# Output projections of a two-layer hybrid kernel: five pairs of tiles in each layer as seven block products instead of eight

## The reference, cut to what matters

```python
for i in range(DEPTH):                       # 2 layers
    y = _even_layer(...) if i % 2 == 0 else _conv_layer(...)   # both end in ... @ w_out
    x = _layernorm(DEEPNORM_ALPHA * x + y, post_ln_g[i], post_ln_b[i])
    x = x + (p[i] @ ple_w[i]) * jax.nn.sigmoid(x @ ple_gate_w[i])
```

## Time and profile before

| what | value |
|---|---|
| median of 3 runs | 2099.53 us (2099.37 to 2099.72) |
| the profiled execution: time | 2099.83 us |
| its span, first to last instruction | 2098.1 us |
| TensorE busy | 2091.8 us |
| VectorE busy | 1256.2 us |
| ScalarE busy | 817.0 us |
| GpSimd busy | 362.0 us |
| DMA, mean over the span | 103 GB/s |

### The profile page before, as it was taken

One profiled execution on the slowest core, in us unless ns is written; L12 is line 12 of the kernel. 1 busy time (PEld: TensorE's weight loads), 2 busy tenths in 40 slices (PEclk: granted clock), 3 DMA queues, 4 the chain that ended last, 5 costly groups with the idle time before them and its releaser, 6 DMA issues.

```text
span 2098.1 us, 28711 instructions
## 1 busy us (share of the span) xinstructions
PE 2091.8 (100%) x10510; PEld 1733.0 (83%) x10510; DVE 1256.2 (60%) x2105; ACT 817.0 (39%) x1042; POOL 362.0 (17%) x196
## 2 busy tenths in 40 slices
...
GB/s 319 141 102 93 70 77 80 80 62 79 81 80 80 60 80 137 133 84 97 99 113 123 135 100 86 96 101 100 100 87 93 100 181 100 92 92 77 142 111 68
DMA packets 33395, 216.76 MB, mean 103 GB/s; under 512 B 3952, under 2 KB 4224, under 8 KB 9520
## 3 DMA queue, kind: packets, MB, share of 16 engines
...
HBM read 207.53 MB, written 8.39 MB: 103 GB/s over the span
## 4 chain that ended last, share of the span: by engine, by line
PE 99%; ACT 1%; DMA 0%; DVE 0%; issue 0%; ACTq 0%
PE G L502 91%; PE X L502 5%; PE T L502 1%; PE T L685 1%; DMA Z<-xT_in 0%; PE T L806 0%; ACT a_hi L917 0%; ACT Z L1112 0%; ACT Y L1184 0%; PE T L811 0%; PE T L657 0%; ACT L1004 0%; DVE tmp L1451 0%; PE T L681 0%; DVE Y L1453 0%
## 5 line engine op out<-in xcount | busy, mean ns | idle before, releaser
L502 PE MATMUL G<-a_hi,w_hi 128*128 128x512 f32 x2764 | 1078.1, 390 | 0.6 <-ACT a_hi L917 0.6
L502 PE MATMUL G<-a_hi,w_lo 128*128 128x512 f32 x2764 | 1072.9, 388 | 0.0
L502 PE MATMUL G<-a_lo,w_hi 128*128 128x512 f32 x2764 | 1070.6, 388 | 0.0
L913 ACT ACTIVATE w_hi<-w_raw 128x2048 fp32r<-128x2048 f32 x173 | 331.5, 1916 | 946.2 <-PE G L502 933.3
L1312 DVE TENSOR_TENSOR w_lo<-w_raw,w_hi 128x2048 fp32r<-128x2048 f32 x128 | 297.1, 2321 | 640.3 <-ACT w_hi L913 640.3
L502 PEld LDWEIGHTS G<-a_hi,w_hi 128*128 128x128 f32 x2764 | 518.9, 188 | 110.3 <-ACT a_hi L917 1.5
L502 PEld LDWEIGHTS G<-a_hi,w_lo 128*128 128x128 f32 x2764 | 518.9, 188 | 107.2 <-issue 0.2
L502 PEld LDWEIGHTS G<-a_lo,w_hi 128*128 128x128 f32 x2764 | 519.0, 188 | 106.4 <-issue 0.5
L1895 DVE SCALAR_TENSOR_TENSOR T<-tmp,par,T 128x512 f32<-128x512 f32 x464 | 306.9, 751 | 0.0
L446 POOL TENSOR_TENSOR w_lo<-w_raw,w_hi 128x2048 fp32r<-128x2048 f32 x45 | 207.8, 4617 | 232.5 <-ACT w_hi L913 232.5
L410 POOL TENSOR_TENSOR a_lo<-Y,a_hi 128x512 fp32r<-128x512 f32 x32 | 44.2, 1397 | 366.9 <-ACT a_hi L917 366.6
...
## 6 DMA issues: line engine op xcount, KB each, us to landing
w_raw<-wall_in SPq DMA_DIRECT2D x174, 1024.0 KB, 4.8
Y<-xT_in POOLq DMA_DIRECT2D x5, 1024.0 KB, 7.2
Y<-w_in POOLq DMA_DIRECT2D x2, 2048.0 KB, 16.0
x_residual<-Y POOLq DMA_DIRECT2D x16, 256.0 KB, 3.8
Y<-x_residual POOLq DMA_DIRECT2D x4, 1024.0 KB, 5.3
out<-Y POOLq DMA_DIRECT2D x15, 256.0 KB, 3.7
w_raw<-wall_in SPq DMA_DIRECT2D x12, 256.0 KB, 7.9
Z<-xT_in SPq DMA_DIRECT2D x6, 512.0 KB, 9.0
```

The lines of the kernel that those rows point to most:

```text
L502: return pe.matmul(o, l, r, start=start, stop=stop)
L913: f(w_hi[:, w.slot, :], w_raw[:, w.slot, :], ACT.Copy).then_inc(S("w_hi"), 1)
```

## The change

Per layer, tiles 0 to 3 are computed as before. Tiles 4 to 13 are taken in five pairs, numbered p = 2 to 6; tiles 14 and 15 (p = 7) are computed in full, but loaded and split in pieces.

In a pair, the first four chunks (`PLAIN_K`) of both tiles are multiplied as before (pieces `r1`, `r2`). The other twelve are seen as 2 x 2 blocks: two tiles by two groups of six chunks on the side of the weights (`b11`, `b21` of the first tile, `b12`, `b22` of the second), two groups of six chunks by two halves of 256 tokens on the side of the activations. The product of such blocks is made with seven products (Winograd's form of Strassen's scheme) instead of eight. It needs four sums of weights, t1 = b11 + b12, t2 = t1 + b22, t3 = b12 + b22 and t4 = t2 + b21, and four sums of activations per chunk (`folds`, made once per layer: three GpSimd instructions, one ScalarE, one VectorE for each of six chunks). Each block product is 18 matmuls of 256 columns.

The sums of weights are made by DMAs that GpSimd issues: one loads the first block, another, with `accum_op=ALU.add`, adds the second to what lies in SBUF. Nine pieces per pair are split (high part by ScalarE, low part by VectorE) into a ring of four slots that lies in `w_hi` and `w_lo`: piece n may be split when the product of piece n-4 is done. t1 lies in `chain`; ScalarE copies it to `later`, where t2 and then t4 are made. The seven products are combined by VectorE out of PSUM with `empty_first`, `empty_products`, `finish_two` and `finish_one`. `piece_low` makes a low part; `high_made`, `low_made`, `summed`, `piece_done` and `emptied` give the semaphore and the value at which that step of a pair is done. `centre_sums` and `square_sums` are the statistics, now for four chunks per pair. Here `half_add` is the addition into `ln_sum`. The last two residual quarters are fetched by ScalarE's DMA queue. `p_raw0` moves from `Z` to `Y` and is loaded later; some buffers change places, and semaphores are merged. The rest of the kernel is as before.

The core of the diff (each piece moved to the left margin):

```diff
+PLAIN_K = 4
+PAIR_K = 6
+HALF_T = T // 2
+QUAD = PAIR_K * P
+FOLD_FROM, FOLD_TO = 2, 7
+FOLDED = ("r1", "r2", "b11", "t1", "t3", "t2", "b22", "t4", "b21")
+UNFOLDED = ("r1", "r2", "b11", "b12", "b21", "b22")
+RING_AT = (3328, 2560, 0, 768)
+CHAIN_AT = 1536
+PIECE_AT = {"r1": (1, 0), "r2": (0, 0), "b11": (1, PLAIN_K * P), "b21": (1, PLAIN_K * P + QUAD),
+            "b12": (0, PLAIN_K * P), "b22": (0, PLAIN_K * P + QUAD)}
...
+folds = rounded("folds", z_at, 0, PAIR_K * 4 * T).rearrange("p (k s n t) -> p k s n t", k=PAIR_K, s=4, n=2)
+fold_sum = nc.alloc_sbuf_tensor_at("fold_sum", [P, HALF_T], F, offset=z_at + 4 * PAIR_K * 4 * T)[:, :]
+chain, other = [nc.alloc_sbuf_tensor_at(n, [P, QUAD], F, offset=at + 4 * CHAIN_AT)[:, :]
+                for n, at in (("chain", w_hi_at), ("other", w_lo_at))]
+w_ring = [[w.rearrange("p s n -> p (s n)")[:, at:at + QUAD] for at in RING_AT] for w in (w_hi, w_lo)]
+fold_raw = [tmp[:, n * 2 * T:(n + 1) * 2 * T].rearrange("p (s t) -> p s t", s=4) for n in range(2)]
+Y4 = Y.rearrange("p (k h t) -> p k h t", k=KC, h=2)
+def piece(name):
+    slot, at = PIECE_AT[name]
+    return w_raw[:, slot, at:at + piece_width(name)]
+later = w_raw[:, 0, PLAIN_K * P:PLAIN_K * P + QUAD]
+def source(p, name):
+    if name[0] != "t":
+        return piece(name)
+    if name == "t3":
+        return tmp[:, 0:QUAD] if p == FOLD_FROM else other
+    return chain if name == "t1" and p > FOLD_FROM else later
+def ring_slot(p, name):
+    return piece_number(p, name) % len(RING_AT)
...
+def ring_free(layer, p, name):
+    n = piece_number(p, name)
+    if n < 2:
+        return S("gemm_done"), W_OUT[layer] + 2 * FOLD_FROM - 1
+    if n < 4:
+        return S("gemm_done"), W_OUT[layer] + 2 * FOLD_FROM
+    return S("piece_done"), layer * (N_PIECES - 1) + n - 3
...
+for p in range(FOLD_FROM + 1, FOLD_TO):
+    sp.wait_ge(*low_made(layer, p - 1, "r1"))
+    load_piece(layer, p, "r1")
+    sp.wait_ge(*low_made(layer, p - 1, "r2"))
+    load_piece(layer, p, "r2")
...
+def fold_operands(layer):
+    for i in range(PAIR_K):
+        first, second = PLAIN_K + i, PLAIN_K + PAIR_K + i
+        if layer == 0:
+            pool.wait_ge(S("y_hgrn"), HEADS)
+        else:
+            pool.wait_ge(S("gated"), second + 1)
+        n = layer * PAIR_K + i
+        if i >= 2:
+            pool.wait_ge(S("fold_lo"), n - 1)
+        raw = fold_raw[i % 2]
+        pool.tensor_tensor(raw[:, 0:2, :], Y4[:, first, :, :], Y4[:, first:second + 1:PAIR_K, 1, :],
+                           ALU.subtract).then_inc(S("fold_step"), 1)
+        pool.wait_ge(S("fold_step"), 2 * n + 1)
+        pool.tensor_tensor(raw[:, 2, :], raw[:, 1, :], Y4[:, first, 0, :], ALU.subtract).then_inc(S("fold_step"), 1)
+        pool.wait_ge(S("fold_step"), 2 * n + 2)
+        pool.tensor_tensor(raw[:, 3, :], raw[:, 2, :], Y4[:, second, 0, :], ALU.add).then_inc(S("fold_raw"), 1)
...
+def add_second(layer, p, name, second):
+    pool.wait_ge(S(f"{name}_landed"), 32 * (layer * N_FOLDS + p - FOLD_FROM) + 16)
+    pool.dma_start(source(p, name), weights_of(layer, p, second), accum_op=ALU.add).then_inc(S(f"{name}_landed"), 16)
+def add_later(layer, p, more):
+    pool.dma_start(later, weights_of(layer, p, more), accum_op=ALU.add).then_inc(S("later_landed"), 16)
+def weight_sums(layer):
+    for p in range(FOLD_FROM, FOLD_TO):
+        if p == FOLD_FROM:
+            pool.wait_ge(S("w_split"), W_OUT[layer] + 2 * p)
+            load_first(layer, p, "t1", "b11")
+            pool.wait_ge(S("fold_lo"), (layer + 1) * PAIR_K)
+            load_first(layer, p, "t3", "b12")
+            add_second(layer, p, "t1", "b12")
+        add_second(layer, p, "t3", "b22")
+        if p > FOLD_FROM:
+            pool.wait_ge(*base_copied(layer, p))
+        pool.wait_ge(*low_made(layer, p, "t1"))
+        add_later(layer, p, "b22")
+        if p + 1 < FOLD_TO:
+            if p == FOLD_FROM:
+                pool.wait_ge(S("gemm_done"), W_OUT[layer] + 2 * p)
+            load_first(layer, p + 1, "t1", "b11")
+        pool.wait_ge(*low_made(layer, p, "t3"))
+        if p + 1 < FOLD_TO:
+            load_first(layer, p + 1, "t3", "b12")
+        pool.wait_ge(*low_made(layer, p, "t2"))
+        add_later(layer, p, "b21")
+        if p + 1 < FOLD_TO:
+            add_second(layer, p + 1, "t1", "b12")
...
+def piece_products(layer, p, name, out, highs, lows, start, stop):
+    pe.wait_ge(*low_made(layer, p, name))
+    hi, lo = [part[ring_slot(p, name)] for part in w_ring]
+    n = len(highs)
+    for k in range(n):
+        at = slice(k * P, (k + 1) * P)
+        mm(out, hi[:, at], highs[k], start and k == 0, False)
+        mm(out, hi[:, at], lows[k], False, False)
+        last = mm(out, lo[:, at], highs[k], False, stop and k == n - 1)
+    return last
...
+piece_products(layer, p, "r1", one[:, :], *whole, True, False).then_inc(done, 1)
+piece_products(layer, p, "r2", two[:, :], *whole, True, False).then_inc(done, 1)
+if p > FOLD_FROM:
+    pe.wait_ge(*emptied(layer, p - 1, 6))
+piece_products(layer, p, "b11", first, *tokens(ones_at, 0), True, True).then_inc(done, 1)
+if p > FOLD_FROM:
+    pe.wait_ge(*emptied(layer, p - 1, 5))
+else:
+    pe.wait_ge(S("fold_lo"), (layer + 1) * PAIR_K)
+piece_products(layer, p, "t1", second[:, HALF_T:T], *fold(1), True, True).then_inc(done, 1)
+piece_products(layer, p, "t3", second[:, 0:HALF_T], *fold(0), True, True).then_inc(done, 1)
+if p == KC // 4:
+    shift(*after("half_summed", 2 * layer, KC // 2 + 2), (ones_r[:, :], sum_high[:, :]))
+pe.wait_ge(*emptied(layer, p, 1))
+piece_products(layer, p, "t2", first, *fold(2), True, True).then_inc(done, 1)
+piece_products(layer, p, "b22", two[:, 0:HALF_T], *fold(3), False, True).then_inc(done, 1)
+piece_products(layer, p, "t4", one[:, HALF_T:T], *tokens(twos_at, 1), False, False).then_inc(done, 1)
+piece_products(layer, p, "b21", one[:, 0:HALF_T], *tokens(twos_at, 0), False, True).then_inc(done, 1)
...
-gemms(w + 2, g + 2, 6)
-gemm(Idx(w + 8), Idx(g + 8))
-shift(*after("half_summed", 2 * layer, KC // 2 + 2), (ones_r[:, :], sum_high[:, :]))
-gemms(w + 9, g + 9, 6)
-gemm(Idx(w + 15), Idx(g + 15))
+gemm_pair(w, g, OPS_OUT[layer], between, pair_lag=OUT_LAG[layer])
+gemm(Idx(w + 2), Idx(g + 2))
+gemm(Idx(w + 3), Idx(g + 3))
+for p in range(FOLD_FROM, FOLD_TO):
+    folded_pair(layer, p)
+pair_in_pieces(layer, FOLD_TO)
...
+if name[0] == "t":
+    act.wait_ge(*summed(layer, p, name))
+else:
+    act.wait_ge(*piece_landed(layer, p, name))
+act.wait_ge(*ring_free(layer, p, name))
+last = (p, name) == (FOLD_TO, UNFOLDED[-1])
+f(w_ring[0][ring_slot(p, name)][:, 0:piece_width(name)], source(p, name), ACT.Copy).then_inc(
+    S("w_hi" if last else "piece_hi"), KC - 2 * FOLD_FROM if last else 1)
...
+piece_high(p, "r2")
+if p > FOLD_FROM:
+    act.wait_ge(*summed(layer, p, "t1"))
+    act.wait_ge(*low_made(layer, p - 1, "t4"))
+    f(later, chain, ACT.Copy).then_inc(S("base_copied"), 1)
+if p == 5:
+    out_square(0)
+    out_square(1)
+piece_high(p, "b11")
+piece_high(p, "t1")
...
+def empty_first(p):
+    dve.wait_ge(*piece_done(layer, p, "b11"))
+    dve.tensor_copy(fold_sum, TB[0][:, 0:HALF_T]).then_inc(S("fold_emptied"), 1)
+def empty_products(p):
+    one, two = 2 * p, 2 * p + 1
+    q6, q7, q5 = TB[0][:, 0:HALF_T], TB[1][:, 0:HALF_T], TB[1][:, HALF_T:T]
+    middle = Y[:, one * T + HALF_T:one * T + 3 * HALF_T]
+    step = S("fold_emptied")
+    dve.wait_ge(*emptied(layer, p, 1))
+    stt(Y4[:, one, 0, :], Y4[:, one, 0, :], ALPHA, fold_sum, op0=ALU.mult, op1=ALU.add).then_inc(step, 1)
+    dve.wait_ge(*piece_done(layer, p, "t3"))
+    stt(middle, middle, ALPHA, TB[1][:, :], op0=ALU.mult, op1=ALU.add).then_inc(step, 1)
+    stt(Y4[:, two, 1, :], Y4[:, two, 1, :], ALPHA, q5, op0=ALU.mult, op1=ALU.add).then_inc(step, 1)
+    dve.wait_ge(*emptied(layer, p, 4))
+    tt(Y4[:, two, 1, :], Y4[:, two, 1, :], q7, ALU.subtract).then_inc(step, 1)
+    dve.wait_ge(*piece_done(layer, p, "t2"))
+    tt(fold_sum, fold_sum, q6, ALU.add).then_inc(step, 1)
+    dve.wait_ge(*emptied(layer, p, 6))
+    tt(Y4[:, one, 1, :], Y4[:, one, 1, :], fold_sum, ALU.add).then_inc(step, 1)
+    tt(Y4[:, two, :, :], Y4[:, two, :, :], fold_sum.unsqueeze(1).broadcast_to([P, 2, HALF_T]),
+       ALU.subtract).then_inc(step, 1)
+def finish_two(p):
+    dve.wait_ge(*piece_done(layer, p, "b22"))
+    dve.wait_ge(*emptied(layer, p, 8))
+    tile = Idx(g + 2 * p + 1)
+    frees(tt(chunk(Y, 2 * p + 1), chunk(Y, 2 * p + 1), out_banks(p)[1][:, :], ALU.add), tile)
+    dve.wait_ge(*drained(tile))
...
+half_sum(1)
+for i in range(PAIR_K):
+    fold_low(i)
+half_sum(2)
+residual_in(1)
...
+p = FOLD_FROM + 1
+lows(p, "r1")
+finish_two(p - 1)
+half_add(5, 4)
+lows(p, "r2", "b11")
+finish_one(p - 1)
+half_add(4, 5)
+lows(p, "t1", "t3", "t2")
+empty_first(p)
+lows(p, "b22", "t4", "b21")
+empty_products(p)
+p = FOLD_FROM + 2
+lows(p, "r1")
+finish_two(p - 1)
+half_add(7, 6)
+lows(p, "r2", "b11")
+finish_one(p - 1)
+half_add(6, 7)
 dve.wait_ge(*after("half_summed", n_ln, KC // 2))
```

(29 more changed lines are left out.)

470 lines of the change are left out of this document (334 added, 136 removed).

## The result

The changed kernel takes 2184.84 us (median of 4 runs, 2180.84 to 2189.11), the kernel before, run beside it, 2099.62 (4 runs, 2099.37 to 2100.44). The ratio is 1.0405, 95% interval 1.0385 to 1.0426: slower by 85.2 us where 47.8 was forecast. The profiled execution took 2184.24, its span is 2182.5.

The account below looks back on a forecast made before the run. Each pair was taken to last max(20.56, 14.1 + 2L) us, bound by VectorE's order with two serial adding DMAs. Pairs 2 to 6 add 21.6, with small terms 23.9 per layer; 2099.8 + 47.8 gives 2147, range 2108 to 2212.

Parts of the forecast that it names:

- The cases of the prediction: Total times by L: main case (0.66) 2134 at 4.05 and 2199 at 7.2; slow adds (0.14) about 2260 at 10.
- L: Time from issue to landing of a 384 KB adding DMA, taken as 4.8 us, with 4.05 to 7.2 as bounds.
- TensorE's gain: Matmul time per pair falls from 21.76 to 20.56 us, 1.20 us per pair, 12.0 us for ten pairs.
- The loop, 14.1 + 2L: Each pair's VectorE order contains two adding DMAs in series, so it lasts 14.1 + 2L us; 23.7 in pair 3.
- Pairs 4, 5 and 6: The loop plus statistics in VectorE's order (centred chunks, square sums): 28.1, 26.8 and 25.4 us.
- Start: Ahead of pair 2, r1's product starts late behind the folds: 1.2 us, plus 0.7 for splits slowed beside GpSimd.
- the last low part at 21.0: End of the folds, in us after tile 2's start, with GpSimd needing 2.9 us per chunk; r1's product then starts at 23.0.
- Pair 2: The pair was to last 26.4 us, as t1's load and adds wait for the folds.
- the load for t3 and the adds come after the folds, so t1's low part starts 7.5 after r1's: In pair 2, t1's low part starts 7.5 us after r1's in place of 4.8, giving 26.4 us.
- 170 GB/s ... above the 103 GB/s mean: The pair's other DMA traffic, some 4 MB in 24 us; the peak is needed only while three adds are issued together.
- The end of the stage: After the last pair, the side input's tiles were to keep covering the remaining work; costed at nothing.
- The clock: Rival, chance 0.03: TensorE's waits drop its clock to 1.2 GHz, 15 us products take twice as long in some pairs; 2250.

Follow-up runs that it names:

- e1: The changed kernel with t2's adding DMA issued before the wait for t1's low part (pair 2 keeps its order); it gained 22.4 us.
- e6: The changed kernel with t2's add early, residual wait behind b21, pair 2's sums issued first, side input and residual quarter loaded and side input split later; 2143.99 us.
- e10: The kernel of e7 with the statistics of chunks 0 to 14 over 8 columns only; 0.75% slower than the kernel before.
- e5: The changed kernel with every adding DMA made a plain one, the additions of weights left out; 2157.03 us.
- e8: The changed kernel with the statistics of chunks 0 to 14 taken over 8 of 512 columns; 2162 us.
- e2: The changed kernel with VectorE's wait for the residual's second quarter moved from ahead of r1 to behind b21; 3 us less than 2184.84.
- e7: The kernel of e6 with two `fold_low` before tile 3's split, pair 2's first loads after the fourth chunk, first side tile split earlier; 2137.13 to 2145.20 us.

## Why the prediction held, and where its size was off

The direction and the mechanism held. The size fell short by 37 us of 85. (The cases of the prediction do not quite follow its own rule of 10 us per layer and us of L: by that they come to 2133, 2196 and 2252, where it has 2134, 2199 and 2260. Nothing hangs on it.)

- *TensorE's gain.* 1.20 us per pair was right: pairs without waits lasted 20.6 to 20.8 (e1, e6, e10), where 20.56 was predicted.
- *The loop, 14.1 + 2L.* 23.7 in pair 3 of both layers, predicted 23.7; L measured 4.79 and 4.74 for 4.8. e1 takes one L out of it and pair 3 falls to TensorE's time; e5 shortens both and the pair follows by the sum.
- *Pairs 4, 5 and 6.* 28.1, 26.8 and 25.4 were predicted; layer 0 had 28.2, 27.2 and 25.6. (Layer 1's pair 4 took 29.8; there t4's add landed in 6.4 us, for 4.7.) Centred chunks and squares in VectorE's order were the right terms (e8, e10).
- *Start: the term was mis-sized, 1.9 for 9.3 and 6.3.* Two parts inside the stage (0.8 of the 9.3 lies ahead of it). The step "the last low part at 21.0" took 2.9 us per chunk, and the trace has 3.76, as GpSimd's 256-column subtraction takes 1.61 us beside VectorE; the earlier trace rows showed such a thing for a split (3.40 for 2.29), and I allowed 0.7 in all. And `residual_in(1)` stands between `half_sum(2)` and r1; the sum passes over it. Its load is issued behind the folds on GpSimd: 3.1 us of TensorE's wait in layer 0, 1.9 in layer 1. e2 shows the one and e7 the other.
- *Pair 2: 26.4 for 33.5 and 31.2.* The step that failed is "the load for t3 and the adds come after the folds, so t1's low part starts 7.5 after r1's", with L kept at 4.8. t1's low part started 11.5 after r1's (869.75 to 881.24), since its add alone took 8.95, and the adds of t2 and t4 took 5.95 and 6.55: 4.0 and 2.9 us too much, 6.9 of the 7.1 in layer 0. I had seen "170 GB/s ... above the 103 GB/s mean" and called it a matter of a short peak. An add weighs more on the engines than its bytes, which the trace of before could not show; e5 removes the addition and pair 2 goes to 23.6.
- *The end of the stage: costed at nothing, cost 3.7 us per layer.* "The side input's tiles" did not cover it. VectorE comes out of pair 7 with statistics undone, and TensorE waits in the side tiles for `Y` (0.92 us) and for a sum in `tmp` (0.67). Another 1.7 us is the clock, which was at the lower level for 3.4 us in both layers:

```profile
1038.02:1041.44 3.42, 3.42 (x9) 2.57 (x9) 2.02 (x7) 0.58 (x2) 0.00 (x0) 0.50 0.00 0
```

In e8's layer 0, without such a stretch, the side tiles last 28.6, with a wait of 1.2 for `tmp`; in its layer 1, with one, 30.1. So of the 2.1 us that narrow statistics seem to save there, 1.7 is the clock.
- *The clock: 0.03 as a rival.* It did not decide, but it has a part: 5.0 us that can be named (1.7 in the side tiles of each layer, 1.6 in pair 7 of layer 1). The other slow stretches of the changed kernel fall into pairs 2, 4, 5 and 6, where TensorE waits behind them anyway. TensorE's timeline at the start of pair 7, after the same wait of 2.8 us, in one fence (layer 0, then layer 1):

```profile
1008.91 0.47 PE L746 MATMUL G<-a_hi,w_hi 128*128 128x512 f32 x1 [2.79 <-DVE w_lo L2157]
1009.22 0.39 PE L746 MATMUL G<-a_lo,w_hi 128*128 128x512 f32 x1
...
1949.12 0.53 PE L746 MATMUL G<-a_hi,w_hi 128*128 128x512 f32 x1 [2.79 <-DVE w_lo L2157]
1949.45 0.63 PE L746 MATMUL G<-a_lo,w_hi 128*128 128x512 f32 x1
...
1952.84 0.39 PE L746 MATMUL G<-a_hi,w_hi 128*128 128x512 f32 x1
```

In layer 1 the matmuls of 512 columns start 0.43 us apart until 1952.84, which is the 1.2 GHz level, and 0.23 apart behind that; the pair's granted clock is 0.93, in layer 0 1.00. Eight matmuls of 0.43 in place of 0.23 are 1.6 us: just the difference between pair 7's 22.4 and 24.0, and between pair 6 in e7 and e6 (22.8 at a granted clock of 1.00, 24.4 at 0.93). This fits the Trainium skill (TensorE: Matmul & The Clock Gate, "A second HAM failure mode: psum-queue depth-cycling") in that idling between groups costs clock; "products of 15 us" at half rate, as the rival had it, did not occur.

The terms that were off come to 7.4 + 7.1 + 3.7 = 18.2 us in layer 0 and 4.4 + 4.8 + 3.7 = 12.9 in layer 1, with 0.9 and 4.2 for pairs 4 to 7: 36.2, against the 36.6 by which the span exceeds the forecast.

Left open: why the same wait lowers the clock in one layer and not in the other; why an adding packet lasts 281 ns; and, of the edges, what the two pairs 2 would take if TensorE never slowed down in them.
